# Overflow branch ahead of the last expert, its down columns in halves with the next norm between them

## The reference, cut to what matters

```python
def moe_swiglu(h, router, w_gate, w_up, w_down):
    ...
    probs = jax.nn.softmax((ht @ router).astype(jnp.float32), axis=-1)
    vals, idx = lax.top_k(probs, TOP_K)                      # 2 of 8 experts for each token
    wts = vals / jnp.sum(vals, axis=-1, keepdims=True)
    gates = jnp.einsum('tk,tke->te', wts, jax.nn.one_hot(idx, N_EXPERTS, dtype=jnp.float32)).astype(h.dtype)
    out = jnp.zeros_like(ht)
    for e in range(N_EXPERTS):
        out = out + gates[:, e:e + 1] * swiglu(ht, w_gate[e], w_up[e], w_down[e])
    return out.reshape(bsz, seq, d)
...
        x = x + moe_swiglu(rmsnorm(x, norm_ffn[i]), ...)     # end of the first block
...
        xn = rmsnorm_2(h, g_mix[l])                          # start of the second
        z = jnp.einsum('bsd,dc->bsc', xn, w_in[l])
```

## Time and profile before

| what | value |
|---|---|
| median of 3 runs | 1267.46 us (1267.12 to 1267.55) |
| the profiled execution | 1267.51 us, span of its profile 1265.7 us |
| TensorE | busy 1194.9 us, 94% of the span |
| VectorE, ScalarE | busy 476.3 us and 449.4 us |
| queue of the weights | packets on it take 67.1% of 16 DMA engines' span |
| TensorE's clock | full but for stretches: mean 0.991 of full speed |

### The profile page before, as it was taken

One profiled execution on the slowest core, in us unless ns is written; L12 is line 12 of the kernel. 1 busy time (PEld: TensorE's weight loads), 2 busy tenths in 40 slices (PEclk: granted clock), 3 DMA queues, 4 the chain that ended last, 5 costly groups with the idle time before them and its releaser, 6 DMA issues.

```text
span 1265.7 us, 18042 instructions
## 1 busy us (share of the span) xinstructions
PE 1194.9 (94%) x7689; PEld 791.3 (63%) x7689; DVE 476.3 (38%) x696; ACT 449.4 (36%) x695; POOL 39.5 (3%) x67
## 2 busy tenths in 40 slices
PE   7999999999999999998999889987899998999998
PEld 6887888888787353343324332432588876888886
DVE  4686555436775200000000000002566654655542
ACT  6546444335765002011000100010576565444430
POOL 4001000000000100000000000010100000000000
PEclk9999999999999999999999999999999999999999
DMA  9637655544437999999999999999753350755430
GB/s 317 236 134 258 216 194 181 180 144 140 165 140 312 407 415 408 407 420 405 421 409 420 406 421 409 420 420 379 269 219 132 133 167 1 244 186 192 177 133 34
DMA packets 89479, 337.51 MB, mean 267 GB/s; under 512 B 6283, under 2 KB 14176, under 8 KB 65728
## 3 DMA queue, kind: packets, MB, share of 16 engines
q1 hardware_dynamic: 85040, 322.35, 67.1%
q0 software_dynamic: 4192, 13.82, 3.1%
q10 hardware_dynamic: 160, 0.07, 0.1%
HBM read 330.71 MB, written 7.74 MB: 267 GB/s over the span
## 4 chain that ended last, share of the span: by engine, by line
PE 76%; DMA 15%; DVE 3%; ACT 2%; issue 2%; SPq 2%; ACTq 0%; DVEq 0%
PE bank L1743 16%; PE bank L1745 16%; PE bank L1744 16%; PE bank L2102 8%; PE bank L2163 6%; PE bank L2108 5%; DMA raw<-in_moe_w_gate 5%; DMA raw_beside<-in_moe_w_up 4%; DMA raw_over_lo<-in_moe_w_up 3%; DMA raw<-in_moe_w_up 2%; SPq L383 2%; PE bank L2180 1%; DMA raw_over_hi<-in_moe_w_down 1%; DVE w_lo L403 1%; PE bank L1855 1%
## 5 line engine op out<-in xcount | busy, mean ns | idle before, releaser
L403 DVE TENSOR_TENSOR w_lo<-raw,w_hi 128x2048 fp32r<-128x2048 f32 (+3 forms) x118 | 258.0, 2200 | 171.9 <-ACT w_hi L398 171.7
L398 ACT ACTIVATE w_hi<-raw 128x2048 fp32r<-128x2048 f32 (+3 forms) x118 | 216.2, 1842 | 168.7 <-PE bank L1745 163.6
L1743 PE MATMUL bank<-w_hi,xT_hi 128*128 128x512 f32 (+2 forms) x672 | 256.8, 382 | 3.6 <-DVE xT_lo L1081 1.7
L1744 PE MATMUL bank<-w_lo,xT_hi 128*128 128x512 f32 (+2 forms) x672 | 253.5, 377 | 0.0
L1745 PE MATMUL bank<-w_hi,xT_lo 128*128 128x512 f32 (+2 forms) x672 | 253.5, 377 | 0.0
L1489 DVE TENSOR_TENSOR e_act<-bank,e_act 128x512 f32<-128x512 f32 x20 | 13.8, 692 | 378.5 <-PE bank L2102 202.3
L1743 PEld LDWEIGHTS bank<-w_hi,xT_hi 128*128 128x128 f32 x672 | 127.1, 189 | 27.6 <-issue 3.5
L1745 PEld LDWEIGHTS bank<-w_hi,xT_lo 128*128 128x128 f32 x672 | 127.0, 189 | 23.0
L1744 PEld LDWEIGHTS bank<-w_lo,xT_hi 128*128 128x128 f32 x672 | 127.1, 189 | 21.9
L1743 PE MATMUL bank<-w_hi,ffn_hi 128*128 128x512 f32 x176 | 69.8, 396 | 0.0
L1744 PE MATMUL bank<-w_lo,ffn_hi 128*128 128x512 f32 x176 | 69.6, 395 | 0.0
(11 more groups left out here) (432 smaller groups left out, 1386.8 us busy)
## 6 DMA issues: line engine op xcount, KB each, us to landing
raw<-in_w_gate_up SPq DMA_DIRECT2D x22, 1024.0 KB, 5.1
raw_over_hi<-in_moe_w_up SPq DMA_DIRECT2D x17, 1024.0 KB, 28.8
raw_over_lo<-in_moe_w_up SPq DMA_DIRECT2D x17, 1024.0 KB, 29.2
raw<-in_moe_w_gate SPq DMA_DIRECT2D x16, 1024.0 KB, 25.6
raw_over_hi<-in_moe_w_gate SPq DMA_DIRECT2D x16, 1024.0 KB, 27.3
raw_over_lo<-in_moe_w_gate SPq DMA_DIRECT2D x16, 1024.0 KB, 28.2
raw<-in_moe_w_down SPq DMA_DIRECT2D x16, 1024.0 KB, 27.6
raw_over_hi<-in_moe_w_down SPq DMA_DIRECT2D x16, 1024.0 KB, 26.0
```

Source lines behind the costliest of these rows:

```text
L398: nc.scalar.activation(w_hi[:, slot, :n], raw[:, slot, :n], ACT.Copy).then_inc(stream.high, 1)
L403: nc.vector.tensor_tensor(w_lo[:, slot, :n], raw[:, slot, :n], w_hi[:, slot, :n].bitcast(F32), ALU.subtract).then_inc(stream.low, 1)
L1743: mm(dst, a_hi, b_hi, start=start, stop=False)
L1744: mm(dst, a_hi, b_lo, start=False, stop=False)
```

## The change

1. The overflow branch moves ahead of the last expert on all engines; its passes count from the seventh expert's end, and all waits of the last expert get a term in the register `over`.
2. The last expert's down pieces become 4 of left columns and then 4 of right ones. The left half is scattered after down 4, not after down 6. After down 5 TensorE transposes blocks 0 and 1 of the next norm; ScalarE and VectorE make their high and low parts before the right half. The left scatter writes banks 2 and 3 instead of 2 and 5.
3. `LAST_SLOTS` changes from up 6 on: down 2 and 3 go to slots 3 and 4 (before 12 and 13), down 4 to 7 to slots 8 to 11 (before 14, 15, 6, 7). So down 4 to 7 wait until up 6, up 7, down 0 and down 1 have been used.
4. ScalarE may split the first fox piece as soon as slots 12 and 13 are free, and loads its table before the left copy to `y`.
5. `REGION_PAD` is 8 words instead of 16: what lies in the region behind it moves by 32 bytes.

```diff
-REGION_PAD = 16
+REGION_PAD = 8
-LAST_SLOTS = (*range(8, 16), *range(2, 8), *range(8, 16), 6, 7)
+LAST_SLOTS = (*range(8, 16), *range(2, 8), 8, 9, 10, 11, 3, 4, 8, 9, 10, 11)
-PUT_BANKS = ((2, 5), (0, 1))
+PUT_BANKS = ((2, 3), (0, 1))
 def by_half(j):
-    return j // 2 % 2, 2 * (j // 4) + j % 2
+    return j // QUARTERS, j % QUARTERS
...
 # SyncE
+                    if p == E - 1:
+                        over = sp.value_load(overflow[0:1, 0:1], min_val=0, max_val=1)
+                        with sp.If(over > 0):
...
                     for c in range(EXPERT_CHUNKS):
-                        load_expert(p * EXPERT_CHUNKS + c, *expert_chunk(A, e, c, p == E - 1))
-                sp.wait_ge(sem("moe_planned"), 1)
-                over = sp.value_load(overflow[0:1, 0:1], min_val=0, max_val=1)
-                with sp.If(over > 0):
...
+                        load_expert(p * EXPERT_CHUNKS + c, *expert_chunk(A, e, c, p == E - 1), over)
 # ScalarE, light_put
                     turned(2, base)
-                    act.wait_ge(W1.used, MOE0 + GU_CHUNKS + 6 + EXPERT_CHUNKS * p)
...
+                    if last:
+                        table(ACT.Sqrt)
+                    act.wait_ge(W1.used, MOE0 + GU_CHUNKS + QUARTERS + EXPERT_CHUNKS * p)
+                    act.wait_ge(sem("moe_rows_stored"), 16 * E)
                     A_(M["y"][:, :HALF], bank[6][:, :], ACT.Copy).then_inc(sem("moe_y"), 1)
+                    if last and "fox" in parts:
+                        norm_high("fox", GAIN_OF["fox"], xT_hi, (0, 1))
                     act.wait_ge(W1.used, MOE0 + EXPERT_CHUNKS + EXPERT_CHUNKS * p)
 # ScalarE, fox
-                table(ACT.Sqrt)
-                act.wait_ge(W1.used, MOE0 + E * EXPERT_CHUNKS + over * (OVERS * EXPERT_CHUNKS))
+                act.wait_ge(W1.used, MOE0 + last_use([12, 13]) + 1 + over * (OVERS * EXPERT_CHUNKS))
                 w2.ahead(-AHEAD)
 # VectorE
-                put_add(E - 1, 0, 0, "moe_added", True)
-                dve.wait_ge(sem("moe_planned"), 1)
-                over = dve.value_load(overflow[0:1, 0:1], min_val=0, max_val=1)
...
+                put_add(E - 1, over * OVERS, 0, "moe_added")
+                dve.wait_ge(sem("moe_added"), 3 + over * (4 * OVERS))
                 V.memset(M["most"][:, 1:2], 0.0).then_inc(sem("x_updated"), 2)
-                put_add(E - 1 + over * OVERS, over * OVERS, 1, "x_updated")
+                if "fox" in parts:
+                    norm_low("fox", GAIN_OF["fox"], xT_lo, xT_hi, None, (0, 1))
+                put_add(E - 1, over * OVERS, 1, "x_updated")
 # TensorE, light_put
-                        if c == 6:
+                        if c == 4:
                             pe.wait_ge(sem("moe_y"), E + 2 * n + 1)
                             for t in range(T):
                                 scatter(0, t)
+                        if c == 5 and last and "fox" in parts:
+                            norm("fox", x, x_ready["fox"], (0, 1))
```

More of the change, by code:

```diff
@@ L368, in over_slot, with landings_in_over, last_use, load_expert @@
             return 2 + c % OVER_RING
-        def load_expert(n, view, k, m):
+        def landings_in_over(slot):
+            return OVERS * (EXPERT_CHUNKS // OVER_RING) if 2 <= slot < 2 + OVER_RING else 0
+        def last_use(slots):
+            return max(n for n in range(E * EXPERT_CHUNKS) if slot_at[n] in slots)
+        def load_expert(n, view, k, m, over=0):
             slot, owner = slot_at[n], owner_before[n]
-            if owner is not None:
+            if owner is not None and owner >= LAST:
+                nc.sync.wait_ge(W1.used, MOE0 + owner + 1 + over * (OVERS * EXPERT_CHUNKS))
+            elif owner is not None:
                 nc.sync.wait_ge(W1.used, MOE0 + owner + 1)
@@ L596, in _ @@
                 pool.wait_ge(sem("moe_rows_stored"), 16 * E)
-                pool.wait_ge(W1.used, MOE0 + 1 + max(n for n in range(E * EXPERT_CHUNKS) if slot_at[n] < 2))
+                pool.wait_ge(W1.used, MOE0 + 1 + last_use([0, 1]))
                 for choice in range(2):
@@ L637, in table, with norm_high @@
                 tables += 1
+            def norm_high(p, gname, hi, blocks):
+                for b in blocks:
+                    act.wait_ge(sem("xT_turned"), before(p, "xT_turned") + b + 1)
+                    for j in range(2):
+                        k = 2 * b + j
+                        ins = A_(hi[:, k, :], bank[NORM_BANKS[p][b]][:, j * S:(j + 1) * S], ACT.Copy, scale=g(gname, k))
+                    ins.then_inc(sem("xT_high"), 1)
             def norm(p, src, ready, gname, hi, ss, rt, between=None, halfway=None):
@@ L642, in norm @@
                     table(ACT.Sqrt)
-                for b in range(4):
+                for b in ((2, 3) if p == "fox" else range(4)):
                     act.wait_ge(sem("xT_turned"), before(p, "xT_turned") + b + 1)
@@ L929, in _ @@
                     heavy(p, base)
-                light_put(E - 1, GROUPS_BEFORE[E - 1], 0, True)
                 act.wait_ge(sem("moe_planned"), 1)
@@ L1074, in used, with norm_low @@
                 dve.wait_ge(w.stream.used, i + 1)
-            def norm_low(p, gname, lo, hi, halfway=None):
-                for b in range(4):
+            def norm_low(p, gname, lo, hi, halfway=None, blocks=range(4)):
+                for b in blocks:
                     dve.wait_ge(sem("xT_high"), before(p, "xT_high") + b + 1)
@@ L1566, in _ @@
                 gates()
-                pick(E - 1)
+                V.memset(M["most"][:, 1:2], 0.0).then_inc(sem("moe_added"), 1)
                 products(0, 0, 0, 3)
@@ L1829, in out_beside, with norm @@
                 return beside, around_last, rest
-            def norm(p, src, ready):
-                for b in range(4):
+            def norm(p, src, ready, blocks=range(4)):
+                for b in blocks:
                     if b in (0, 2):
@@ L2217, in landed @@
                         more = 0 if i is None else 16 * (2 * EXPERT_CHUNKS // EXPERT_RING) * i
+                        if over is not None and landings_in_over(slot_at[n]):
+                            more = over * (16 * landings_in_over(slot_at[n]))
                         pe.wait_ge(expert_landed[slot_at[n]], 16 * landing_at[n] + more)
```

119 lines of the change are left out of this document (66 added, 53 removed).

## The result

The changed kernel takes 1255.32 us (median of 5 runs, 1254.69 to 1256.76) against 1267.46 us (5 runs, 1266.36 to 1268.93): ratio 0.9904, 95% interval 0.9892 to 0.9917, so 12.1 us less. The prediction said 1261.2 us, 6.3 us less, with a range that ended at 1259.8. The direction was right, and so were the steps forecast for the end of the last expert, which gave 6.5 us in the trace. The size was not: the pad, which the prediction had put at 0, gave another 3.8 us, and a slow stretch of the clock far behind the change fell away.

A forecast was written before the change was run, and what follows sets the result against it. TensorE, busy 94% of the span, was taken as the bound. Savings of 3.45 (issue), 1.7 (clock), 0.8 (norm) and 0.4 (down pieces), less 0.1 for register instructions, took 1267.5 to 1261.2 us; range 1259.8 to 1264.2.

The forecast's parts named there:

- The branch leaves the end: Before the last expert's right scatter: TensorE's issue gap goes (3.45 us), and the scatter runs at full clock (1.7 us).
- Half of the norm: Between second sum and first fox matmul: norm blocks 0 and 1 done before the right sums, saving 0.8 us.
- Down pieces: Last expert's down product: reordered pieces with transposes between them let the right copy start 0.4 us earlier, at 893.34.
- ScalarE: First fox piece's high part: ready 0.95 us before VectorE wants it; 0.75 us late with the old table load.
- The branch's new place: Last expert's start: jump delays gate 0 by 5.9 us to 836.7, caught up by up 4; no cost.
- The slots: Down 4 to 7: waiting for slots issues the last two 4 us later; taken as nothing, upper bound 3.0 us.
- my bounds: Landing times for the last down pieces: lower 6.8 us, a lone piece; upper 13.5 us, the transfer's own.
- two rivals built on late landings: Last expert: down pieces come late, 1264.2 us, chance 0.08; or its loads starve, 1268.9 us, chance 0.04.
- The pad: Addresses of the region's tiles, moved by 32 bytes: effect taken as 0, with 0.43 us to either side.
- The sum at the place: Last expert's end to first fox matmul: 6.4 us saved, less 0.1 us for register instructions, 6.3 us.
- a slow stretch gone: An earlier 1.2 GHz stretch disappears: with cover of everything, the likeliest case's lower edge, 1260.0 us.
- the rival with starved loads: Last expert's loads: late issues mean late landings, down 7 8.5 us late; 1268.9 us, slower, chance 0.04.

The follow-up runs named there:

- after_nohalves: Changed kernel with down pieces, left scatter and norm back in their old order (halves alternating, whole norm behind the right sum): 1257.73 us, ratio 0.9926.
- after_pad16: Changed kernel with REGION_PAD back at 16 words: 1259.12 us, ratio 0.9942.
- pad24: Kernel before the change with REGION_PAD 24 instead of 16: 1266.47 us, ratio 0.9995.
- ffnpad: Kernel before the change with 8 unused words ahead of ffn_hi, moving only ffn_hi and ffn_lo by 32 bytes: 1265.87 us, ratio 0.9993.
- ffn24: Kernel before the change with 24 words ahead of ffn_hi, moving only ffn_hi and ffn_lo: 1266.16 us, ratio 0.9996.
- ffnhi24: Kernel before the change with 24 words ahead of ffn_hi and 8 ahead of ffn_lo: 1267.23 us, ratio 1.0007.
- all32: Kernel before the change with an 8-word tile ahead of all others and REGION_PAD 8, so all operands start at 160 mod 512: 1262.7 us, ratio 0.9961.
- ffn120: Kernel before the change with 120 words ahead of ffn_hi, putting ffn_hi and ffn_lo at 128 mod 512: 1262.86 us, ratio 0.9963.
- ffn56: Kernel before the change with 56 words ahead of ffn_hi, putting ffn_hi and ffn_lo at 384 mod 512: 1262.85 us, ratio 0.9962.
- after_oldslots: Changed kernel with the last expert's pieces back in their old ring slots: 1255.91 us, ratio 0.992.
- pad8: Kernel before the change with only REGION_PAD set to 8 instead of 16: 1261.99 us, ratio 0.9961.
- before_nobranch: Kernel before the change without the overflow loop and its flag on all engines: 1261.78 us, ratio 0.9959.
- after_nobranch: Changed kernel without the overflow loop and its flag on all engines: 1256.24 us, ratio 0.9914.
- latetable: Changed kernel with ScalarE's table load back behind the copy of the right half: 1256.55 us, ratio 0.9916.
- zaligned: Changed kernel with 24 words behind the memory attention's small tiles, moving z, fqT, fkT, mkT, mq, mqT to 128 mod 512: 1255.96 us, ratio 0.9921.
- after_xT32: Changed kernel with xT_hi and xT_lo moved from 128 to 160 mod 512, weights and region staying at 128: 1265.02 us, ratio 0.999.

## Why the prediction was off, step by step

- **The branch leaves the end** (3.45 + 1.7): right. The issue fell from 3.51 to 0.04 us and the scatter from 3.67 to 2.00, at full clock. Taken alone the step gives 4.7 us from down 7 on; the rest comes only together with ScalarE's table and piece.
- **Half of the norm** (0.8): right, 0.8 in the traces of after and after_nohalves. By time it is 2.4 us with intervals that overlap, which I don't read as more.
- **Down pieces** (0.4 earlier): right. The copy starts at 892.10 where 893.34 was forecast, but all matmuls before the place came 1.3 us earlier than in before (the pad in conv and ffn1, less the later start); without these it is 893.4.
- **ScalarE** (cover 0.95, late by 0.75 with the old table load): right. The high part ends at 894.50 and VectorE wants it at 895.53, a cover of 1.03; with the late table it waits, for some 0.5.
- **The branch's new place** (gate 0 at 836.7, covered): right. Gate 0 starts at 835.57, or 836.9 with those 1.3 us, at half clock; and taking the branch away gains nothing. SyncE needs 8.66 us from the issue before gate 0 to gate 0's (2.84 in before), and yet no gate piece was waited for.
- **The slots** (0): right, though an issue took 0.54 us and not 2.4, so down 7 went out at 878.69 and not at 880.9. The median issue to landing was 8.9 and 10.3 us for these pieces, between my bounds. Neither of the two rivals built on late landings came up.
- **The pad** ("I take 0 and, for want of a row, the spread of the three runs, 0.43 us, to either side"): this step failed, a term put at nothing without a reason. It is worth 3.8 us (after_pad16 against after): 528 ffn matmuls at 0.0065 us make 3.4, the second product of conv 0.4. The bound was no bound, since the spread of repeated runs of one program says nothing of what another address does. With the 3.8 the sum would have been 1257.4 us. A row that should have warned me stood in the trace of before: two forms alike in all but the tile, at 391 and 395 ns, 0.227 and 0.233 us from start to start. It says that something in the region may cost up to 768 matmuls (528 of ffn, 96 of yT, 96 of memT, 48 of cT) 6 ns each, 4.8 us, and the pad is the one edit that moves the region. By it the range of the pad had to reach down to -4.8. That another address slows the region further no row of before priced, and at the distances tried later (32 to 160) none did.
- **The sum at the place**: 6.3 forecast, 6.5 found.
- **What else went**: a stretch of 1.2 GHz from 1054.9 us in before, in the mem attention, which is not in after. Its matmuls cost 1.15 us more there:

```profile
1055.00:1058.00 3.00, 3.00 (x11) 2.38 (x10) 0.78 (x3) 0.78 (x4) 0.00 (x0) 0.50 0.02 5
```

It is there in the profiles of before, pad24, ffnpad, ffn24, ffnhi24, all32, ffn120, ffn56 and after_oldslots, and absent in after, pad8, pad16, before_nobranch, after_nobranch, nohalves, latetable, zaligned and after_xT32. It doesn't follow any one edit (after_oldslots has it, after not; before_pad8 lacks it, before_all32 has it); what sets it stays open. The prediction allowed for a slow stretch gone, but only as the lower edge of a case, not beside a gain from the pad.

A small slip in the sums: behind down 7 the forecast saves 5.98 us by its own terms (11.94 to 5.96), not the 6.05 of the rival with starved loads. Nothing hangs on it.

6.5 at the place, 3.8 by the pad, 1.15 by the clock and 0.1 in fox make 11.55; the profiled execution of after began 0.8 us later, which leaves the 10.75 measured. The medians differ by 12.1; the 1.4 between is within the spread of the runs (2.6 us before, 2.1 after). The run with the old pad agrees: after_pad16 is 0.9942 (0.9929 to 0.9956) of before, 7.3 us less (5.6 to 9.0), and 6.5 and 1.15 make 7.65.

## What to carry to other kernels

An edit that only moves addresses is not free by default: ask of every matmul form whether the same shape runs at two speeds with different tiles, and give such an edit the difference times the count as its range, down for tiles that run slow and up for tiles that run fast (after_xT32 lost 9.7 us by 32 bytes). Where TensorE streams matmuls like these without a gap, let the stationary and the moving tile start at the same byte mod 256. And a stop of one engine is best put where it waits for landings anyway: the same 6.1 us jump cost over 4 us at the end of a stage and nothing that showed at the start of a stage bound by its loads.

## What the runs showed of the hardware that I had not expected

- The pace of back-to-back float32r matmuls (128x128 stationary, 512 columns) is 0.2268 to 0.2272 us if the two operands start at the same byte mod 256 in their partitions, and 0.2324 to 0.2333 at distances of 32, 64 and 128 bytes, 2.3 to 2.9% more. The rows for the weight load don't show it (188 ns in both). Distances of 96, 160 and more were not tried with both split parts alike, and why it is so (a conflict between the load and the stream, for one) was not measured.
- An absolute border did not matter: both operands at 160 are as fast as both at 128 (before_all32), and a stationary tile on a 128-byte border is slow if the moving one is 128 bytes off (before_ffn24).
- A taken jump over the overflow loop takes 6.127 us at its new place and 6.151 at the old one; SyncE's issue of a 1 MB piece took 0.33 to 0.55 us for the first five behind its stop (from 802.95) and for down 4 to 7, but 2.07 us at 794.29 and 6.36 us at 805.77, the sixth behind the stop. That the length of its queue decides this is argued, not shown.
